# The turns between layers: post-norm row applied at PSUM by VectorE, modulation in token layout, an earlier square of tile 1

## The reference

```python
# layer 0 (GLA) and layer 1 (NSA)
h = rms_norm(x, pre_norm[i])
y = mixer(h, ...)                      # its last step is a product with w_out
x = x + rms_norm(y, post_norm[i])
...
# the hybrid layer starts with
mod = silu(c) @ w_ada + b_ada
shift, scale, gate = split(mod, 3)
h = rms_norm(x, norm_gain) * (1 + scale) + shift
proj = h @ w_in
```

## Time and profile before

| | |
|---|---|
| median of 3 runs | 1354.02 us (1354.02 to 1354.82) |
| profiled execution, its own time | 1353.65 us |
| span of its instructions | 1351.8 us |
| TensorE matmul busy | 1286.2 us, 95% |
| TensorE weight load busy | 1057.1 us, 78% |
| VectorE busy | 640.0 us, 47% |
| ScalarE busy | 579.3 us, 43% |
| GpSimd busy | 398.1 us, 29% |
| mean granted TensorE clock | 0.976 of full speed |

### The profile page before, as it was taken

One profiled execution on the slowest core, in us unless ns is written; L12 is line 12 of the kernel. 1 busy time (PEld: TensorE's weight loads), 2 busy tenths in 40 slices (PEclk: granted clock), 3 DMA queues, 4 the chain that ended last, 5 costly groups with the idle time before them and its releaser, 6 DMA issues.

```text
span 1351.8 us, 19527 instructions
## 1 busy us (share of the span) xinstructions
PE 1286.2 (95%) x7898; PEld 1057.1 (78%) x7898; DVE 640.0 (47%) x1024; ACT 579.3 (43%) x1102; POOL 398.1 (29%) x196
## 2 busy tenths in 40 slices
PE   6999998988799999999997999999999999999998
PEld 5799876886697766656697978787877888888898
DVE  6372144677942646788736233333333283101534
ACT  4535213533223126688756244434454411434333
POOL 1444401213354311110020332222222354444432
PEclk9999998998799999999998999999999999999999
DMA  5322202633656331110012222222222132233221
GB/s 179 112 94 71 85 1 66 216 98 125 208 142 118 63 78 32 32 33 1 2 32 63 67 90 63 63 63 63 63 64 63 32 124 94 90 97 109 94 94 63
DMA packets 130208, 109.67 MB, mean 81 GB/s; under 512 B 36162, under 2 KB 127424, under 8 KB 130128
## 3 DMA queue, kind: packets, MB, share of 16 engines
q1 hardware_dynamic: 130128, 108.54, 27.2%
HBM read 106.43 MB, written 2.10 MB: 80 GB/s over the span
## 4 chain that ended last, share of the span: by engine, by line
PE 72%; issue 14%; DVE 6%; POOL 4%; ACT 3%; DMA 0%; POOLq 0%; DVEq 0%; ACTq 0%
PE banks L1142 32%; PE banks L1133 8%; PE banks L1165 5%; POOL w_lo L558 4%; PE banks L1681 3%; PE banks L1542 3%; PE banks L1576 3%; PE banks L1561 2%; PE banks L1230 2%; PE banks L1646 2%; PE banks L1599 2%; PE banks L1695 1%; PE banks L1428 1%; DVE ada_sum L1892 1%; PE banks L1413 1%
## 5 line engine op out<-in xcount | busy, mean ns | idle before, releaser
L558 POOL TENSOR_TENSOR w_lo<-raw,w_hi 128x1024 fp32r<-128x1024 f32 x158 | 386.5, 2467 | 849.5 <-ACT w_hi L634 849.3
L1142 PE MATMUL banks<-act_hi,w_hi 128*128 128x512 f32 x704 | 280.6, 399 | 4.6 <-POOL w_lo L558 4.6
L1142 PE MATMUL banks<-act_hi,w_lo 128*128 128x512 f32 x704 | 275.9, 392 | 0.0
L1142 PE MATMUL banks<-act_lo,w_hi 128*128 128x512 f32 x704 | 275.8, 392 | 0.0
L634 ACT ACTIVATE w_hi<-raw 128x1024 fp32r<-128x1024 f32 x168 | 168.2, 1051 | 144.9 <-PE banks L1142 89.2
L1142 PEld LDWEIGHTS banks<-act_hi,w_hi 128*128 128x128 f32 x704 | 133.2, 189 | 35.0 <-issue 7.7
L1142 PEld LDWEIGHTS banks<-act_hi,w_lo 128*128 128x128 f32 x704 | 133.3, 189 | 28.3 <-issue 1.4
L1142 PEld LDWEIGHTS banks<-act_lo,w_hi 128*128 128x128 f32 x704 | 133.1, 189 | 28.3
L1133 PE MATMUL banks<-w_hi,act_hi 128*128 128x256 f32 x384 | 109.8, 286 | 0.0
L1133 PE MATMUL banks<-w_lo,act_hi 128*128 128x256 f32 x384 | 109.4, 285 | 0.0
L1133 PE MATMUL banks<-w_hi,act_lo 128*128 128x256 f32 x384 | 109.3, 285 | 0.0
(11 more groups left out here) (364 smaller groups left out, 2512.7 us busy)
## 6 DMA issues: line engine op xcount, KB each, us to landing
raw<-w_in SPq DMA_DIRECT2D x32, 1024.0 KB, 5.6
raw<-gla_w_in SPq DMA_DIRECT2D x13, 1024.0 KB, 5.3
ada_raw<-w_ada SPq DMA_DIRECT2D x8, 1024.0 KB, 6.3
raw<-nsa_w_in SPq DMA_DIRECT2D x32, 256.0 KB, 4.5
raw<-nsa_w_in SPq DMA_DIRECT2D x7, 1024.0 KB, 6.8
raw<-gla_w_out SPq DMA_DIRECT2D x4, 1024.0 KB, 8.4
ada_first<-w_ada SPq DMA_DIRECT2D x4, 1024.0 KB, 8.0
raw<-nsa_w_out SPq DMA_DIRECT2D x16, 256.0 KB, 4.5
```

Source lines behind the costliest of these rows:

```text
L558: pool.tensor_tensor(w_lo[:, u, k], raw[:, u, k], w_hi[:, u, k].bitcast(F32), ALU.subtract).then_inc(lo_done, 1)
L1142: mm = pe.matmul(b[:], w[:, u, k, m * P:(m + 1) * P], x[:, k, :], start=(k == 0 and n == 0), stop=(k == KT - 1 and n == 2))
```

## The change

- ScalarE no longer copies y out of PSUM. It squares, and raises `y_squared`; VectorE then multiplies the bank by the post-norm row into y (`y_weighted`, 128 x 512; `own_weighted`, 128 x 256) and frees the bank. So `bank_free` of the chunks c0 to c3 comes from VectorE.
- `y_added` is one instruction: x = y * root + x.
- Turn 1 modulates like turn 0 scales: x * root * gain row, plus shift row, two instructions of 128 x 1024 ahead of the turning (`modulated`). TensorE makes the two rows (16 matmuls of a broadcast column with the identity into banks 4 to 7) just ahead of `out_and_turn(1, ...)`; the second row, in banks 6 and 7, waits for `pv_read` at NPAIR. VectorE copies the rows to SBUF (`mod_rows`) after the split of the gated output. `gain_mod` is made earlier, ahead of the first query turn.
- Both turns share `high_turned`, `low_turned` and one order on VectorE (`norm_and_turn`). ScalarE squares tile 1 (`x_rooting(1)`) ahead of `take_two(2, 1)`.
- VectorE's order ahead of turn 0: wait for both rows, weight the two banks of c0, `ada(0, 2)`, then `norm_and_turn`, and `ada(2, 2)` after it.

```diff
@@ ScalarE, out_and_norm
                 def take_two(j, m):
...
-                    act.activation(y[:, 2 * m:2 * m + 2, j * CW:(j + 1) * CW], bank[b].rearrange("p (t n) -> p t n", t=2), ACT.Copy)
                     for t in range(2):
                         last = squares(j, 2 * m + t, bank[b][:, t * CW:(t + 1) * CW])
-                    last.then_inc(bank_free[b], 1)
+                    last.then_inc(y_squared, 1)
                 def take_own(t):
                     act.wait_ge(y_full, TT * i + t + 1)
-                    zone = own_bank(c3, t)[:, 0:CW]
-                    squares(3, t, zone)
-                    act.activation(y[:, t, 3 * CW:4 * CW], zone, ACT.Copy).then_inc(y_taken, 1)
-                    act.wait_ge(y_taken, TT * i + t + 1)
+                    link(squares(3, t, own_bank(c3, t)[:, 0:CW]))
+                    act.sem_inc(y_squared, 1)
                     y_rooting(t)
...
                 x_rooting(0)
+                x_rooting(1)
                 take_two(2, 1)
-                x_rooting(1)
                 next_weights(c3 + 1)
@@ TensorE, ahead of out_and_turn(1, ...)
+            pe.wait_ge(gain_ready, 1)
+            for row, col in enumerate((gain_mod, mod)):
+                if row == 0:
+                    pe.wait_ge(t_high, NUNIT)
+                else:
+                    pe.wait_ge(pv_read, NPAIR)
+                for k in range(KT):
+                    mm = pe.matmul(bank[4 + 2 * row + k // 4][:, k % 4 * P:(k % 4 + 1) * P],
+                                   col[:, k:k + 1].broadcast_to([P, P]), ident[:], start=True, stop=True)
+                mm.then_inc(mod_row_full, 1)
             out_and_turn(1, C_NOUT, ot_low, 0, y_tok2)
@@ VectorE
+            def y_weighted(i, c0, j, m, y, row):
+                c = c0 + j
+                b = 2 * (c % 2) + m
+                dve.wait_ge(y_squared, 10 * i + (2 * j + m + 1 if j < 2 else (5, 8)[m]))
+                dve.tensor_tensor(y[:, 2 * m:2 * m + 2, j * CW:(j + 1) * CW], bank[b].rearrange("p (t n) -> p t n", t=2),
+                                  row[:, j * CW:(j + 1) * CW].rearrange("p (o n) -> p o n", o=1).broadcast_to([P, 2, CW]),
+                                  ALU.mult).then_inc(bank_free[b], 1)
+            def own_weighted(i, c3, t, y, row):
+                dve.wait_ge(y_squared, 10 * i + (6, 7, 9, 10)[t])
+                link(dve.tensor_tensor(y[:, t, 3 * CW:4 * CW], own_bank(c3, t)[:, 0:CW], row[:, 3 * CW:4 * CW], ALU.mult))
+                dve.sem_inc(y_taken, 1)
...
-                link(dve.scalar_tensor_tensor(y[:, t], y[:, t], y_root[:, t:t + 1], row, ALU.mult, ALU.mult))
-                dve.tensor_tensor(x_tok[:, t], x_tok[:, t], y[:, t], ALU.add).then_inc(x_updated, 1)
+                dve.scalar_tensor_tensor(x_tok[:, t], y[:, t], y_root[:, t:t + 1], x_tok[:, t], ALU.mult,
+                                         ALU.add).then_inc(x_updated, 1)
...
+            def norm_and_turn(i, c0, y, row, scaled_rows):
+                c3 = c0 + 3
+                y_weighted(i, c0, 1, 0, y, row)
+                y_weighted(i, c0, 1, 1, y, row)
+                y_weighted(i, c0, 2, 0, y, row)
+                own_weighted(i, c3, 0, y, row)
+                y_added(i, 0, y)
+                own_weighted(i, c3, 1, y, row)
+                y_added(i, 1, y)
+                scaled_rows(0)
+                scaled_rows(1)
+                y_weighted(i, c0, 2, 1, y, row)
+                low_turned(i, c3, 0)
+                own_weighted(i, c3, 2, y, row)
+                next_low(c3 + 1, 0)
+                next_low(c3 + 1, 1)
+                low_turned(i, c3, 1)
+                y_added(i, 2, y)
+                own_weighted(i, c3, 3, y, row)
+                y_added(i, 3, y)
+                next_low(c3 + 2, 0)
+                scaled_rows(2)
+                next_low(c3 + 2, 1)
+                scaled_rows(3)
+                low_turned(i, c3, 2)
+                low_turned(i, c3, 3)
+
-            ada(0, 3)
             dve.wait_ge(rows_landed, 32)
...
-            ada(3, 1)
+            y_weighted(0, C_GOUT, 0, 0, y_tok, rows1[:, 0])
+            y_weighted(0, C_GOUT, 0, 1, y_tok, rows1[:, 0])
+            ada(0, 2)
+            norm_and_turn(0, C_GOUT, y_tok, rows1[:, 0], pre_scaled)
+            ada(2, 2)
...
+            def modulated(t):
                 dve.wait_ge(x_rooted, TT + t + 1)
+                link(dve.scalar_tensor_tensor(y_tok2[:, t], x_tok[:, t], x_root[:, t:t + 1], mod_rows[:, 0], ALU.mult,
+                                              ALU.mult))
+                dve.tensor_tensor(y_tok2[:, t], y_tok2[:, t], mod_rows[:, 1], ALU.add).then_inc(xn_ready, 1)
```

More of the change, by code:

```diff
@@ L105, in build_program @@
         silu_c = sb("silu_c", [P, KT])
+        gain_mod = sb("gain_mod", [P, KT])
         tmp = sb("tmp", [P, 2, S])
@@ L257, in build_program @@
         x_updated, x_rooted, xn_ready, xn_turned = sem("x_updated"), sem("x_rooted"), sem("xn_ready"), sem("xn_turned")
-        hs_ready, hi_tile, h_tile = sem("hs_ready"), sem("hi_tile"), sem("h_tile")
+        y_squared, hi_tile, h_tile = sem("y_squared"), sem("hi_tile"), sem("h_tile")
+        gain_ready, mod_row_full, mod_row_ready = sem("gain_ready"), sem("mod_row_full"), sem("mod_row_ready")
         gate_row_full, gate_row_ready, x_part = sem("gate_row_full"), sem("gate_row_ready"), sem("x_part")
@@ L692, in y_rooting, with out_and_norm @@
                 root_of(y_sum, y_root, t).then_inc(y_rooted, 1)
-            def out_and_norm(i, c0, y, junk, high):
+            def out_and_norm(i, c0, y, junk):
                 c2, c3 = c0 + 2, c0 + 3
@@ L739, in out_and_norm @@
                 x_rooting(0)
+                x_rooting(1)
                 take_two(2, 1)
-                x_rooting(1)
                 next_weights(c3 + 1)
-                high(0)
+                high_turned(i, c3, 0)
                 take_own(2)
-                high(1)
+                high_turned(i, c3, 1)
                 take_own(3)
-                act.wait_ge(y_taken, TT * i + TT)
-                for b in (2 * (c3 % 2), 2 * (c3 % 2) + 1):
-                    act.sem_inc(bank_free[b], 1)
                 next_weights(c3 + 2)
@@ L752, in out_and_norm, with high_turned @@
                 x_rooting(3)
[L753 to L759, removed]
+                high_turned(i, c3, 2)
+                high_turned(i, c3, 3)
+            def high_turned(i, c3, t):
+                act.wait_ge(xn_turned, TT * i + t + 1)
+                for half, b in enumerate(turn_banks(c3, t)):
                     last = act.activation(by_tile(act_hi, t)[:, 4 * half:4 * half + 4], bank[b].rearrange("p (k n) -> p k n", k=4),
@@ L1901, in take_mod, with y_added @@
                                   ALU.add).then_inc(mod_ready, 1)
-            def y_added(i, t, y, row):
+            def y_weighted(i, c0, j, m, y, row):
[9 more added lines that the diff above has]
+                dve.sem_inc(y_taken, 1)
+                if t == TT - 1:
+                    for b in (2 * (c3 % 2), 2 * (c3 % 2) + 1):
+                        dve.sem_inc(bank_free[b], 1)
+            def y_added(i, t, y):
                 dve.wait_ge(y_rooted, TT * i + t + 1)
-                link(dve.scalar_tensor_tensor(y[:, t], y[:, t], y_root[:, t:t + 1], row, ALU.mult, ALU.mult))
-                dve.tensor_tensor(x_tok[:, t], x_tok[:, t], y[:, t], ALU.add).then_inc(x_updated, 1)
+                dve.scalar_tensor_tensor(x_tok[:, t], y[:, t], y_root[:, t:t + 1], x_tok[:, t], ALU.mult,
+                                         ALU.add).then_inc(x_updated, 1)
             def next_low(c, part):
@@ L1918, in pre_scaled, with low_turned @@
                                          ALU.mult).then_inc(xn_ready, 1)
-            def low_turned(t):
-                dve.wait_ge(hi_tile, t + 1)
-                for half, b in enumerate(turn_banks(C_GOUT + 3, t)):
+            def low_turned(i, c3, t):
+                dve.wait_ge(hi_tile, TT * i + t + 1)
+                for half, b in enumerate(turn_banks(c3, t)):
                     k = slice(4 * half, 4 * half + 4)
@@ L2085, in pair_out @@
                 dve.tensor_tensor(o, o, bank[6][:, 0:P], ALU.add).then_inc(pv_read, 1)
+            link(dve.scalar_tensor_tensor(gain_mod[:], mod[:, KT:2 * KT], 1.0, vec[:, VAT["gain2"]:VAT["gain2"] + KT],
+                                          ALU.add, ALU.mult))
+            dve.sem_inc(gain_ready, 1)
             turn_sum(6, lambda m: qT[:, m])
@@ L2124, in _ @@
             split_gated(KT - 1)
[L2125 to L2129, removed]
-                dve.wait_ge(x_rooted, TT + t + 1)
[L2132 to L2147, removed]
-            dve.wait_ge(rows_landed, 48)
[L2150 to L2169, removed]
+            for row in range(2):
+                dve.wait_ge(mod_row_full, row + 1)
+                for half in range(2):
+                    last = dve.tensor_copy(mod_rows[:, row, half * S:(half + 1) * S], bank[4 + 2 * row + half])
```

(3 more changed lines are left out.)

28 lines of the change are left out of this document (6 added, 22 removed).

## The result

The changed kernel takes 1355.29 us in the median of 20 runs (1353.59 to 1358.59), the kernel before 1353.28 us in the median of its 20 runs beside it (1351.39 to 1356.34). The ratio is 1.0021, 95% interval 1.0015 to 1.0028: 2.8 us slower (2.0 to 3.8), just over the 0.2% that I took as what can be told from no change. The profiled execution took 1355.29 us by its own time, with a span of 1353.5 us and a mean granted clock of 0.979; that of before took 1353.65. I forecast 1356.6 and +2.6 us.

A forecast was written before the change was run, and what follows sets the result against it. TensorE, holding 72% of the span, was taken as the bound. Turn 0's +6.2 us and turn 1's -3.6 us gave +2.6 on 1353.65, or 1356.25; with 0.37 for the median, 1356.6. Eight-in-ten range: 1349.5 to 1360.5.

The forecast's parts named there:

- The wait at `own_tile(c3, 0)`, 7.7 us: Turn 0: TensorE waits 7.7 us for the bank, freed only after `ada(0, 2)` and `y_weighted(1, 0)` on VectorE.
- Rival 1: Turn 0: GpSimd doesn't block VectorE in `ada(0, 2)`, TensorE waits 2.1 us, -5.9 us in all, 1348; 15%.
- Its lower clock, 2.9 us: Turn 0: after the 7.7 us stop TensorE's lower clock costs 2.9 us, bounds 1.3 and 2.9.
- Turn 0 in all, +6.2 us: Turn 0: new wait and lower clock, less the saved waits and their lower clock, sum to +6.2 us.
- Turn 1's start, +7.5 us: Ahead of turn 1: delay for `pv_read` 4.9, eight matmuls 1.8, lower clock 0.8: +7.5 us, bounds 4.9 and 7.9.
- The turn, -11.4 us: Turn 1 after its start: shorter `h_tile` waits and less lower clock, less a new tile 2 wait: -11.4 us.
- Rival 3: Both turns: the two remaining 1.5 us waits lower the clock, +1.75 each, or VectorE's order lengthens them: +6, 1360; 15%.
- Rival 2: Both turns: the stops cost no lower clock; turn 0 +3.3, turn 1 -6.2, together -2.9 us, 1351; 10%.
- The sum: Whole kernel: turn 0 +6.2 and turn 1 -3.6 give +2.6 us, forecast 1356.6 us.

The follow-up runs named there:

- the fifth experiment: The kernel before with only `x_rooting(1)` moved ahead of `take_two(2, 1)` in ScalarE's order: 1347.68 us, ratio to the kernel before 0.9968.
- the third experiment: The changed kernel with `pair_out(NPAIR - 1)` at step 0 of the gating loop, not step 7: 1348.94 us, ratio to the kernel before 0.9964.

## Why the prediction was right, and where it was off

The direction, the size and both new waits came out as forecast; the terms one by one:

- **The wait at `own_tile(c3, 0)`, 7.7 us.** 7.77, 7.94 and 7.76 in three executions. The row landed at 243.2, 0.9 sooner than I took, and TensorE was there at 251.2, 0.8 sooner, so the length held. What is shown by experiment is that the `ada` instructions ahead of the bank on VectorE's queue are the wait: with both blocks moved ahead it is gone, with one moved behind it is half, and the time follows. That GpSimd stretches them is read from traces (9.9 and 4.0 us for the same block, here and in the earlier trace rows); no run took GpSimd away at this place. The working had one VectorE instruction pass for each of GpSimd's; the trace has 2.30 and then, in the chain, 2.54 and 2.50. The Trainium skill (SBUF — State Buffer, Who interferes with whom) says that a VectorE instruction with two SBUF inputs contends with GpSimd's reads, that one with at most one SBUF input does not as long as it is outside the 2-port modes, and that `tensor_scalar` can enter such a mode; my prediction left this exception out. The trace agrees for two inputs (2.54 and 2.50 us for 0.515) and for a PSUM operand (0.69 us beside GpSimd). The TENSOR_SCALAR at 244.46 has one large input and took 2.30 us for 0.35. It may be the exception: from 256 to 1024 columns a TENSOR_SCALAR goes from 0.35 to 0.76 us, 0.53 ns for each column more, a SCALAR_TENSOR_TENSOR from 0.515 to 1.28, 1.0 ns, so the first runs at twice the rate. But its small operand, `silu_c`, lies in SBUF too, and no run here tells which of the two it is. Rival 1 (VectorE not blocked) is refuted.
- **Its lower clock, 2.9 us.** This term was too large: 1.4 in the profiled execution. It measured 1.4, 1.7 and 2.3 us behind stops of 7.8 to 7.9 us, and 2.4 behind 3.85. So the bounds that I had, 1.3 to 2.9, hold, and the value can't be read from the length of the stop, which is how I chose it. The 2.9 was misread as well: I set 8.66 us against 48 x 0.12 = 5.74, but 48 matmuls at full clock behind a wait take 6.02 in the same view, so the stop of 6.97 had cost 2.6. The Trainium skill (TensorE: Matmul & The Clock Gate, What's actually happening) says of a kernel's start that the number of slow matmuls differs from run to run; these four stops inside a kernel agree.
- **Turn 0 in all, +6.2 us.** +3.9 in the trace. Taken between starts of TensorE's instructions, the terms are 7.9 (the wait) + 1.4 (its clock) + 0.2 (`h_tile` 2, 1.68 for 1.40) - 0.7 - 2.5 - 1.6 = +4.7, and 0.8 less because c2's weights came 0.8 us sooner in this trace. Of the 2.3 us too many, 1.5 are the clock's term. The 0.59, the 2.36 and its lower clock are gone as forecast.
- **Turn 1's start, +7.5 us.** The second row's matmuls began 0.34 us behind the start of `pair_out`, as forecast (5.86 us of stop for 6.0). Its matmuls and c0's took 2.0 and 1.1 us more than at full clock, 3.1 for the 2.6 that I took. c0 ends at 705.71 for 693.62, 12.1 us later; 4.0 of it are turn 0's, so the start costs +8.1.
- **The turn, -11.4 us.** From c0's end to the first head score it is 87.1 us for 98.4 (705.71 to 792.8, 693.62 to 792.0): -11.3. The wait for `h_tile` 2 is 1.49 us at full clock, the one ahead of tile 2 0.73 (0.8 to 1.0 forecast), the one for `h_tile` 4 is gone. Two small errors cancel: the lower clock behind `h_tile` 2, which goes, was worth 2.6 us and not 2.9, and the new wait is 0.3 us shorter than the 1.0 that I added. Rival 3 (the waits of 1.5 us lower the clock) didn't happen: 1.00 in the window at 744. Rival 2 (no lower clock at all) is refuted by the 0.50 at 258 and 690.
- **The sum.** +2.6 forecast, +2.8 by the runs, +1.6 by the own times of the two profiled executions. The two waits and their causes were foreseen; that the total is met within 0.2 us is in part luck. The terms miss by more than the sum: turn 0 was 2.3 too high and the start of turn 1 0.6 too low, and the stretch behind the turns, which I counted at nothing, has 0.9 in the traces. The +2.8 also holds a second group of slower runs (below), of which the prediction knew nothing.

**The 0.9 us behind the turns.** The last product's 384 matmuls take 45.07 us in the kernel before and in the fifth experiment, and 46.1 in the changed kernel and in every other experiment, that without the rows and that with the rows alone included. So it comes neither from the rows nor from the weighting at PSUM, but from something that all the kernels made out of the changed one share. They share the new place of the buffer `gain_mod`, which is declared earlier; whether it is that, no run tells.

What the change did, by its parts: alone on the kernel before, the earlier square gives 4.3 us and the rows cost 3.3, about 1.0 of it in the last product; that the wait for `pv_read` is what makes them late shows in the trace (5.86 us) and in the third experiment. The post-norm at PSUM was not run alone, and its share can't be had by subtraction, since the parts don't add up: the square and the rows shorten the same wait for `h_tile` 2 (6.97 us, to 4.53 and to 0.70), and with the rest of the change in place the rows cost nothing that can be told (0.9950 with them, 0.9964 without).

Open: the changed kernel's 20 runs lie in two groups, 11 from 1353.6 to 1355.3 us and 9 from 1356.6 to 1358.6. The varying price of the lower clock at two places is of that size (1.4 to 2.3, 1.7 to 3.1). The mean granted clock of each run is on record: 0.976 to 0.981 in the lower group, 0.975 to 0.978 in the upper, which points that way but overlaps. Both traces are of the lower group, so this is only argued.

## What to carry to other kernels

When an engine takes over the job of freeing a buffer, everything that stands ahead on its queue becomes part of the wait for that buffer: here a filler that had cost nothing (16 instructions of `ada`) cost 9.6 us, and moving it by three lines into the idle time ahead of a DMA gave it all back. Time such fillers beside the other engines that will be running, not alone: the same six instructions took 3.09 and 7.13 us. And when a change saves time in the middle of a stage, look at what it adds to the stage's start: the rows saved 7 us only once the event that they wait for was moved ahead; both moves together beat the kernel before by 1.0 to 1.2% where the change as it stood lost 0.2%.

## What the runs showed of the hardware

- The price of the lower clock doesn't follow the length of the stop: 2.4 us behind 3.85 us, 1.4, 1.7 and 2.3 behind 7.8 to 7.9; behind 2.36 us about 1.5 in the kernel before and nothing behind 2.35 in the fifth experiment; while behind the stops of 1.4 to 1.7 us for `h_tile` 2 the next 48 matmuls ran at full clock (6.01 and 6.02 us).
- Short products are hit as well: eight fp32 matmuls of a 128 x 128 identity took 3.47 and 3.79 us behind the stop of 5.86 us, and 1.78 to 1.95 at full clock.
- Beside a stream of GpSimd subtractions with two SBUF inputs, a TENSOR_SCALAR on VectorE with one large SBUF input and a column took 2.30 us for 0.35, a SCALAR_TENSOR_TENSOR 2.5 us for 0.515, and a product of a PSUM bank with an SBUF row its usual 0.69.
- At the same granted clock of 1.00, the same 384 matmuls of 256 columns took 45.07 us in one kernel and 46.1 in another (0.117 and 0.120 us each). Why is open.
